# A chunked RWKV-7 inverse: its turned form kept by a product and a masked copy at each level, and three token turns put together

## The reference

```
S_t = S_{t-1} diag(w_t) + (S_{t-1} a_t) b_t^T + v_t k_t^T ;  y_t = S_t r_t
a_t = -kk_t,  b_t = kk_t * a_rate_t
```

## Time and profile before

| what | value |
|---|---|
| median of 3 runs | 3205.87 us (3204.98 to 3208.65) |
| the profiled execution | 3205.82 us, span 3204.0 us |
| PE busy | 3145.8 us (98%) |
| DVE busy | 2132.3 us (67%) |
| ACT busy | 1459.1 us (46%) |
| granted TensorE clock, mean | 0.998 |
| loop over the pairs | 2496 to 2690 us of the span |

### The profile page before, as it was taken

The page is one execution under the profiler, slowest core; times in us unless marked ns, Lnnn a source line. Parts: engine busy times, 40 slices in busy tenths (PEclk is TensorE's granted clock), DMA queues, the critical chain, the costliest instruction groups (busy, mean ns, idle before and its releaser), DMA issues.

```text
span 3204.0 us, 52305 instructions
## 1 busy us (share of the span) xinstructions
PE 3145.8 (98%) x22626; PEld 2696.1 (84%) x22626; DVE 2132.3 (67%) x2715; ACT 1459.1 (46%) x1993; POOL 136.3 (4%) x134
## 2 busy tenths in 40 slices
PE   9999999999999999999999999999999999999998
PEld 7887787888889988988899887998777777799886
DVE  6546766775389835363898458995666655799637
ACT  3357644443255523432555345554336564355424
POOL 2100000000000001000100011000120000100002
PEclk9999999999999999999999999999999999999999
DMA  5311232232323223222232332322223000133331
GB/s 183 115 53 66 91 107 80 92 102 90 105 86 106 96 98 114 95 88 92 84 102 97 106 105 80 106 102 91 85 81 103 16 4 16 66 106 106 105 100 65
DMA packets 47236, 287.03 MB, mean 90 GB/s; under 512 B 6416, under 2 KB 6688, under 8 KB 21408
## 3 DMA queue, kind: packets, MB, share of 16 engines
q1 hardware_dynamic: 44960, 279.51, 25.6%
q0 software_dynamic: 2048, 4.20, 0.5%
HBM read 277.39 MB, written 2.10 MB: 87 GB/s over the span
## 4 chain that ended last, share of the span: by engine, by line
PE 80%; DVE 5%; ACT 2%; issue 1%; POOL 0%; DVEq 0%; ACTq 0%
PE ps L527 42%; PE ps L2850 8%; PE ps L2872 7%; PE ps L2871 7%; PE ps L2870 7%; PE ps L4192 3%; PE ps L4230 1%; PE ps L1251 1%; DVE wl L344 1%; ACT wh L328 1%; PE ps L1252 1%; PE ps L1253 1%; DVE xl L3666 0%; PE ps L3282 0%; DVE tmp L3674 0%
## 5 line engine op out<-in xcount | busy, mean ns | idle before, releaser
L344 DVE TENSOR_TENSOR wl<-raw,wh 128x2048 fp32r<-128x2048 f32 (+2 forms) x215 | 434.2, 2020 | 328.4 <-ACT wh L328 328.1
L527 PE MATMUL ps<-xl,wh 128*128 128x512 f32 (+1 forms) x1312 | 503.6, 391 | 3.0 <-POOL xl L3563 3.0
L328 ACT CAST wh<-raw 128x2048 fp32r<-128x2048 f32 (+2 forms) x212 | 356.9, 1683 | 292.0 <-PE ps L527 263.7
L527 PE MATMUL ps<-xh,wh 128*128 128x512 f32 x1056 | 416.5, 395 | 13.0 <-DVE xl L3666 3.4
L527 PE MATMUL ps<-xh,wl 128*128 128x512 f32 x1056 | 390.2, 392 | 0.2 <-DVE wl L344 0.2
L527 PEld LDWEIGHTS ps<-xl,wh 128*128 128x128 f32 (+1 forms) x1312 | 245.8, 187 | 56.7 <-POOL xl L3563 3.8
L527 PEld LDWEIGHTS ps<-xh,wh 128*128 128x128 f32 x1056 | 197.8, 187 | 66.2 <-issue 16.3
L527 PE MATMUL ps<-hid_r,wh 128*128 128x512 f32 x640 | 249.0, 389 | 0.0
L527 PEld LDWEIGHTS ps<-xh,wl 128*128 128x128 f32 x1056 | 197.5, 187 | 44.6 <-issue 1.0
L2870 PE MATMUL ps<-terms_h,sums_h 128*128 128x256 f32 x768 | 217.3, 283 | 0.0
L2871 PE MATMUL ps<-terms_l,sums_h 128*128 128x256 f32 x768 | 217.3, 283 | 0.0
(11 more groups left out here) (570 smaller groups left out, 7720.1 us busy)
## 6 DMA issues: line engine op xcount, KB each, us to landing
raw<-in_up SPq DMA_DIRECT2D x88, 1024.0 KB, 4.9
raw<-in_down SPq DMA_DIRECT2D x64, 704.0 KB, 4.0
raw<-in_up_c SPq DMA_DIRECT2D x22, 1024.0 KB, 4.9
raw<-in_down_c SPq DMA_DIRECT2D x16, 704.0 KB, 4.0
raw<-in_gates SPq DMA_DIRECT2D x8, 1024.0 KB, 4.8
raw<-in_gv SPq DMA_DIRECT2D x8, 1024.0 KB, 4.8
raw<-in_gu SPq DMA_DIRECT2D x8, 1024.0 KB, 4.8
raw<-in_gout SPq DMA_DIRECT2D x8, 1024.0 KB, 4.9
```

What stands on the lines that cost most here:

```text
L328: nc.scalar.copy(wh[:, slot, 0:w], raw[:, slot, 0:w]).then_inc(hi_ready, 1)
L344: nc.vector.tensor_tensor(wl[:, slot, 0:w], raw[:, slot, 0:w], wh[:, slot, 0:w].bitcast(F32), ALU.subtract).then_inc(lo_ready, 1)
L527: last = nc.tensor.matmul(out, stationary, moving, start=(fresh and q == 0), stop=(t == kt - 1 and half == per - 1 and q == 2), skip_group ...
```

## The change

The turned form `xt_` is no longer made anew at each level. Level 0 still turns X with four transposes, and ACT copies it. At levels 1 to 4, behind `dx`, PE makes the turned addition as well, `dt` = `z_` turned times `xt_` (16 products of 64x64, by feature, into bank 2), and DVE adds it to `xt_` by a masked copy with turned masks (`add_turned`). ACT's copies of `xt` at levels 1 to 4 and PE's transposes there are gone. `dx` of level n now waits for `turned{n-1}`, and `z` waits for `add{n-1}`, which the transposes did before it. In PE's list `z4` moves ahead of `tokens_v`, so that `tokens_v`, `tokens_k` and `tokens_a` follow each other. Four turned masks are added to the table `wmask`, which is fetched by two DMAs in place of one.

```diff
-    wm = [s < t, s <= t, s == t] + [level(s, t, 1 << n) for n in range(6)]
+    wm = [s < t, s <= t, s == t] + [level(s, t, 1 << n) for n in range(6)] + [level(t, s, 1 << n) for n in range(1, 5)]
...
+        turned_masks = area("turned_masks", [P, 4, C], 83 * KB)
-        masks_here = fetch([(reset[:, :], io["reset"]), (masks[:, :, :].rearrange("p m c -> p (m c)"), io["wmask"]),
+        masks_here = fetch([(reset[:, :], io["reset"]), (masks[:, :, :].rearrange("p m c -> p (m c)"), io["wmask"][:, 0:9 * C]),
+                            (turned_masks[:, :, :].rearrange("p m c -> p (m c)"), io["wmask"][:, 9 * C:13 * C]),
...
+        def where_turned(m):
+            return turned_masks[:, m, :].bitcast(I32).unsqueeze(1).broadcast_to([P, NC, C])
...
+            def add_turned(m, n):
+                need(dve, pB, m, f"dt{n}")
+                mark(nc.vector.copy_predicated(blocks(xt_), where_turned(n - 1), blocks(ps[:, bank["xt"], :])), vB, f"turned{n}")
...
                 add_x(m, 1)
+                add_turned(m, 1)
                 bonus(m)
                 add_x(m, 2)
+                add_turned(m, 2)
...
                 add_x(m, 3)
+                add_turned(m, 3)
...
                 add_x(m, 4)
+                add_turned(m, 4)
...
-                turned_x(m, 0)
+                turned_x(m)
...
-                turned_x(m, 1)
...
-                turned_x(m, 2)
...
-                turned_x(m, 3)
...
-                turned_x(m, 4)
...
             def z(m, n):
                 if n == 1:
                     need(pe, aA, m, "ab")
                     if m:
                         need(pe, vB, m - 1, "add5")
+                else:
+                    need(pe, vB, m, f"add{n - 1}")
                 products(pB, f"z{n}", feature_half("z"), (by_token, ab, by_token, xs_[m % 2]))
 
             def dx(m, n):
                 need(pe, aB, m, f"z{n}")
+                if n > 1:
+                    need(pe, vB, m, f"turned{n - 1}")
                 products(pB, f"dx{n}", token_half("dx"), (by_feature, xt_, by_feature, z_))
+
+            def dt(m, n):
+                products(pB, f"dt{n}", lambda e, c: by_feature(ps[:, bank["xt"], :], e, c), (by_feature, z_, by_feature, xt_))
...
                 dx(m, 1)
+                dt(m, 1)
                 if behind:
                     ends_x(m - 1)
-                xt(m, 1)
                 z(m, 2)
                 bonus(m)
                 if behind:
                     ends_y(m - 1)
                 dx(m, 2)
+                dt(m, 2)
                 if ahead:
                     spread(m + 1)
-                xt(m, 2)
                 z(m, 3)
                 if behind:
                     ends_n(m - 1)
                 dx(m, 3)
+                dt(m, 3)
                 if behind:
                     ends_r(m - 1)
+                z(m, 4)
                 if ahead:
                     tokens_v(m + 1)
-                xt(m, 3)
-                z(m, 4)
-                if ahead:
                     tokens_k(m + 1)
                     tokens_a(m + 1)
...
                 dx(m, 4)
+                dt(m, 4)
                 if ahead:
                     tokens_b(m + 1)
                     gram_a(m + 1)
...
-                xt(m, 4)
                 z(m, 5)
```

More of the change, by code:

```diff
@@ L3855, in rwkv @@
         vA = Named(sem("grams_vector"), ["x0", "rb_t", "ak_t", "rk_t", "bonus"], KD, lead=True)
-        vB = Named(sem("levels_vector"), ["add1", "add2", "add3", "add4", "add5"], KD, lead=True)
+        vB = Named(sem("levels_vector"), ["add1", "turned1", "add2", "turned2", "add3", "turned3", "add4",
+                                          "turned4", "add5"], KD, lead=True)
         vC = Named(sem("ends_vector"), ["r_new", "m"], KD, lead=True)
@@ L3859, in rwkv @@
         aA = Named(sem("grams_scalar"), ["eye", "k_v", "b_a", "ab", "akv"], KD, lead=True)
-        aB = Named(sem("levels_scalar"), ["xt0", "z1", "xt1", "z2", "xt2", "z3", "xt3", "z4", "xt4", "z5"], KD, lead=True)
+        aB = Named(sem("levels_scalar"), ["xt0", "z1", "z2", "z3", "z4", "z5"], KD, lead=True)
         aC = Named(sem("ends_scalar"), ["new", "n", "y0"], KD, lead=True)
@@ L3863, in rwkv @@
         pS = Named(sem("spread_tensor"), ["spread"], KD, lead=True)
-        pB = Named(sem("levels_tensor"), ["xt0", "z1", "dx1", "xt1", "z2", "dx2", "xt2", "z3", "dx3", "xt3", "z4", "dx4", "xt4", "z5",
+        pB = Named(sem("levels_tensor"), ["xt0", "z1", "dx1", "dt1", "z2", "dx2", "dt2", "z3", "dx3", "dt3", "z4", "dx4", "dt4", "z5",
                                           "dx5"], KD, lead=True)
@@ L4111, in z, with turned_x @@
                 mark(nc.scalar.activation(of_chunks(z_), in_halves("z"), ACT.Copy), aB, f"z{n}")
-            def turned_x(m, n):
-                need(act, pB, m, f"xt{n}")
-                if n == 0 and m:
+            def turned_x(m):
+                need(act, pB, m, "xt0")
+                if m:
                     need(act, pB, m - 1, "dx5")
-                mark(nc.scalar.copy(xt_, ps[:, bank["xt"], :]), aB, f"xt{n}")
+                mark(nc.scalar.copy(xt_, ps[:, bank["xt"], :]), aB, "xt0")
             def ends(m):
@@ L4287, in weighted, with xt @@
                          order=ONE_BY_ONE)
[L4289 to L4294, removed]
+            def xt(m):
+                need(pe, vA, m, "x0")
+                turned(pB, "xt0", xs_[m % 2], bank["xt"])
             def z(m, n):
@@ L4346, in pair_tensor @@
                 grams_k(m)
-                xt(m, 0)
+                xt(m)
                 z(m, 1)
```

## The result

The changed kernel takes 3218.65 us (median of 6 runs, 3216.93 to 3220.75); the kernel before 3205.43 (6 runs). The ratio is 1.004, with a 95% interval of 1.003 to 1.005. The forecast was 3213.5, slower; the direction and the range held, the range by 0.35 us; the forecast move of 7.7 us was a little more than half of the 13.2 that came.

A forecast was written before the change was run, and what follows sets the result against it. PE was taken to bound the middle pairs: six times (1.12 + 0.10) gives 7.3 us, plus 0.1 for the first pair and 0.3 for the last, +7.7 on 3205.8, so 3213.5 us; range 3207 to 3219.

The forecast's parts named there:

- What bounds: In the six middle pairs PE's throughput sets the period; a shorter chain of dependences is worth nothing there.
- The removed sets, the steps and the price of `dt`: PE, each middle pair: transposes and steps removed save 2.60 us, four `dt` at 0.93 add 3.72, net +1.12.
- The first rival: `dt` runs at the pace of `dx`, 0.54 us, on PE: 12.5 us less, 3201.0; 12%.
- The third: PE overlaps more than summed, or the breaks of 0.38 and 0.17 shrink: six times 0.55 less, 3210.2; 12%.
- the break of 0.38: PE's wait before `weighted`, at the end of five DVE instructions in a row; claimed to stay as it is.
- What the moves uncover: Next pair's `grams_b` waits on ACT's copy of the turned b and a, with less PE work meanwhile: 0.1 a pair.
- DVE: Four more masked copies a pair, +2.5 us; margins about 0 (level 3), 0.1 to 0.2 (level 4), 0.2 (`first_x`); cost nothing.
- The second rival: DVE becomes late at level 3, level 4 or `first_x`, up to 0.6 in seven pairs: +4.2, 3217.7; 14%.
- First and last pair: Loop's end pairs, where PE waits more: `dt` partly fills waits, other levels lose; about +0.1 first, +0.3 last.
- The waits of 0.86 and 0.83: PE's waits at level 1 of the first pair and level 2 of the last; `dt1` and `dt2` fill them.
- Tables: Mask table in two DMAs delays what is queued behind on SP; cost nothing, 0.5 us without cover.
- The fourth rival: 896 more products bring more stalls with no releaser on PE, one more in each pair: +4, 3217.5; 4%.

The follow-up runs named there:

- `z4` put back: The changed kernel with `z4` back behind `tokens_v`: 3218.37 us (5 runs), ratio to the kernel before 1.0037.
- doubling: The changed kernel with each `dt` made twice, the second time over the first in the same bank: 3252.89 us (one run).
- the two runs with two banks: Neighbouring products written to different banks: `weighted` on the changed kernel, 3219.36 us; `weighted` and `ends_x` on the kernel before, 3206.09 us.
- the run with one product: The changed kernel with only the first of the 16 products of each `dt`, all waits and DVE copies kept: 3198.41 us (one run).
- one word: The kernel before with `weighted` waiting for the masked ak it reads instead of the masked rk: 3202.23 us against 3206.49, ratio 0.9987.
- the one kernel whose densest 16 us had 31.5 starts a us: The changed kernel with each `dt` replaced by one product of 512 columns into the same bank: 3217.56 us (5 runs), ratio 1.0038.

## Why the prediction came out as it did

**What bounds.** Right. PE sets the middle pairs, and taking ACT's copies and the dependences away gained nothing there.

**The removed sets, the steps and the price of `dt`.** Right. The sum had PE's work at +1.12 a middle pair; it grew by 6.82 / 6 = 1.14. A middle pair was to take about 23.5, and without a stall it takes 23.77. The steps of 0.08 were confirmed by `z4` put back (0.14 for two). The 0.93 was taken from `weighted`; doubling gave 0.98. The rule in the Trainium skill, "TensorEngine Tiling (Array Packing)", section "Restrictions and Gotchas", that different row tiles can't access one PSUM bank at the same time, pointed to the right price. In the two runs with two banks the time got no shorter and the pace stayed (1.61 for `weighted` with `dx1`), so they don't bear out the bank as the reason. The first rival (12%) fell with the price. The third (12%) fell too: the break of 0.38 stayed, and the one of 0.16 to 0.17 grew to 0.24.

**What the moves uncover.** The wait of `grams_b` for the copy of b and a was put at 0.1; it is 0.12 a pair. One wait was overlooked: `tokens_a` of the next pair needs bank 4, and so the `m` of the pair behind, which DVE makes in the same pass of the loop. DVE comes to it later now, and PE waits 0.07 a pair on average, 0.4 in all. The wait before `z1` grew from 0.16 to 0.24, 0.5 in the middle pairs, where I had said that it stays.

**DVE.** Right as costed, with margins of 0, 0.27 and 0.54 where I had 0, 0.1 to 0.2 and 0.2. The second rival was closer than its 14% says: the run with one product shows DVE as the bound 2.4 us below the period after.

**First and last pair.** I had +0.1 and +0.3; they came to +0.5 and +1.7. Of the last, 0.9 is stalls (1.3 against 0.4). The waits of 0.86 and 0.83 went as said, so the rest lies in levels that I priced at what a middle pair loses.

**Tables.** Right: what is ahead of the loop isn't longer.

**The term that was mis-sized** in the sum is the one for stalls without a releaser. I had them at no change and gave more of them a rival of 4%, at +4 us. They were +3.1 (4.2 against 1.1). The trace of before has two long ones, 0.52 and 0.42 in the last pair, and I gave them no price; with 896 more products they should have been a term of the sum. The range held by luck: its upper part was meant for a `dt` of 1.08 or a late DVE, and neither came. The fourth rival, with 4% and 3217.5, is the one whose mechanism came, on top of the sum. Put together, in the profile: PE's work 6.8, stalls in the middle pairs 2.2 (2.9 against 0.7), the waits on DVE and ACT there 1.6, the first pair 0.5, the last 1.7, ahead of the loop -0.6; 12.2 in all. The median moved by 13.2; the 1.0 between is within the spread of the runs.

## What to carry to other kernels

A step that is moved off the dependence chain gains nothing where one engine is already full: count its work, with the switches between kinds of product, before its latencies. Here four 128x128 transposes cost PE less (0.59 to 0.67 us) than sixteen 64x64 products that stay on two quarters of the array (0.93), and where both operands lie by the same halves of the partitions as the result, no order of the products changes that. Look in such a loop for a wait on a result that isn't read; one word gained 4.3 us here, where the whole rearrangement lost 13.2. And where PE stalls with no releaser, set the stalls beside the instruction transfers before they are called chance.

## What the runs showed of the hardware that was not expected

Sixteen 64x64 single-precision products (32 instructions) on two quarters take 0.92 to 0.98 us, and 0.92 whether neighbours write one bank or two; going round all four quarters they take 0.54. A step from small products to 128x128 ones and back costs 0.14 to 0.16. PE stalls with no releaser of up to 1.5 us each appear when its instructions are dense, and none appeared in the one kernel whose densest 16 us had 31.5 starts a us. All 66 over 0.15 us end 1.2 to 1.6 us after a 16 KB transfer of instructions has ended. Taking out a break of 0.38 us in PE's work shortened the period by 0.60 (22.36 to 21.76).
